# A delta-rule branch whose score matrices are kept in one orientation, the later token's factor moved into level masks and into the small substitutions

## What is computed

```
lhs = I + beta[l] * (k[l] . k[m]) * decay(l, m)     for l later than m, else 0 off the diagonal
sol = lhs^-1 [ beta * v | beta * gamma * k ]        (unit lower triangular solve)
u   = u0 - w @ state
o   = gamma * (q @ state) + (qk * decay) @ u
state = gamma_last * state + kd^T @ u
```

## Time and profile before

| | us |
|---|---|
| median of 3 runs | 805.44 |
| lowest, highest | 804.22, 806.6 |
| the profiled execution | 806.24 |
| its span, first to last instruction | 804.4 |
| PE busy | 748.4 (93%) |
| DVE, ACT, POOL busy | 341.6, 256.1, 300.7 |
| mean granted TensorE clock | 0.996 |

### The profile page before, as it was taken

How to read it: one execution, slowest core, us unless ns; L and a number is a source line. 1 busy time by engine, 2 the same in 40 slices (tenths; PEclk the granted TensorE clock), 3 DMA queues, 4 the chain that set the end, 5 groups by cost and what they waited for, 6 DMA issues and landing times.

```text
span 804.4 us, 14079 instructions
## 1 busy us (share of the span) xinstructions
PE 748.4 (93%) x5523; PEld 598.3 (74%) x5523; DVE 341.6 (42%) x805; ACT 256.1 (32%) x462; POOL 300.7 (37%) x346
## 2 busy tenths in 40 slices
PE   5999999999999999999999999979999999988784
PEld 5887788788878877888888887857767776665551
DVE  6466643285684861435415333651222112211125
ACT  5343232361633767322305255511111111111012
POOL 2774525441520452254444254333333333322111
PEclk9999999999999999999999999999999999999998
DMA  9956742510220522474385294499999999999975
GB/s 250 162 110 124 218 124 53 104 42 13 53 53 20 136 56 53 98 216 96 83 176 169 60 320 183 180 358 375 390 385 389 390 393 387 380 386 387 390 300 219
DMA packets 74346, 166.60 MB, mean 207 GB/s; under 512 B 18838, under 2 KB 46310, under 8 KB 66344
## 3 DMA queue, kind: packets, MB, share of 16 engines
q1 hardware_dynamic: 65856, 150.34, 58.9%
q0 software_dynamic: 5392, 9.61, 3.6%
q10 hardware_dynamic: 3032, 5.74, 2.3%
HBM read 156.98 MB, written 16.97 MB: 216 GB/s over the span
## 4 chain that ended last, share of the span: by engine, by line
PE 58%; DMA 26%; DVE 9%; issue 2%; POOL 2%; ACT 1%; SPq 1%; ACTq 0%; DVEq 0%; POOLq 0%
DMA arena<-in_w_exp_up 24%; PE bank L1075 13%; PE bank L1077 12%; PE bank L1076 12%; PE bank L1068 12%; PE bank L1424 3%; DMA arena<-y_half 1%; PE bank L1434 1%; PE bank L1116 1%; DVE rows L1864 1%; DVE rows L1863 1%; PE bank L1226 1%; DVE h_lo L1836 1%; DVE hT L1908 1%; DMA rt<-in_norm_ffn_g 1%
## 5 line engine op out<-in xcount | busy, mean ns | idle before, releaser
L876 POOL TENSOR_TENSOR ring_low<-ring,w_high 128x512 fp32r<-128x512 f32 (+1 forms) x64 | 81.4, 1272 | 117.2 <-ACT w_high L1516 113.1
L1075 PE MATMUL bank<-h_hi,w_high 128*128 128x512 f32 x296 | 119.5, 404 | 0.0
L1076 PE MATMUL bank<-h_lo,w_high 128*128 128x512 f32 x296 | 115.8, 391 | 0.0
L1424 PEld LDWEIGHTS bank<-arena,hT 128*64 128x64 f32 x1728 | 96.6, 136 | 24.7 <-issue 12.5
L1424 PE MATMUL bank<-arena,hT 128*64 128x128 f32 x1728 | 100.7, 274 | 8.7 <-DMA arena<-in_w_exp_up 6.7
L876 POOL TENSOR_TENSOR w_low<-ring,w_high 128x512 fp32r<-128x512 f32 x56 | 75.9, 1355 | 59.1 <-ACT w_high L1516 54.9
L2182 DVE SCALAR_TENSOR_TENSOR rt<-rt,bank 128x128 f32<-128x128 f32 x32 | 9.2, 288 | 175.3 <-ACT rt L1749 175.3
L1516 ACT ACTIVATE w_high<-ring 128x2048 fp32r<-128x2048 f32 (+1 forms) x32 | 58.7, 1836 | 58.5 <-PE bank L1077 39.3
L1077 PE MATMUL bank<-h_hi,ring_low 128*128 128x512 f32 x168 | 66.6, 396 | 0.0
L1075 PEld LDWEIGHTS bank<-h_hi,w_high 128*128 128x128 f32 x296 | 55.7, 188 | 14.5 <-issue 3.5
L1076 PEld LDWEIGHTS bank<-h_lo,w_high 128*128 128x128 f32 x296 | 55.7, 188 | 11.0
(11 more groups left out here) (330 smaller groups left out, 1313.8 us busy)
## 6 DMA issues: line engine op xcount, KB each, us to landing
arena<-in_w_exp_gate SPq DMA_DIRECT2D x27, 1024.0 KB, 13.3
arena<-in_w_exp_up SPq DMA_DIRECT2D x27, 1024.0 KB, 17.0
arena<-in_w_exp_down SPq DMA_DIRECT2D x27, 1024.0 KB, 19.2
ring<-in_w_in SPq DMA_DIRECT2D x33, 512.0 KB, 6.6
ring<-in_w_exp_gate SPq DMA_DIRECT2D x5, 1024.0 KB, 13.8
ring<-in_w_exp_up SPq DMA_DIRECT2D x5, 1024.0 KB, 17.3
ring<-in_w_exp_down SPq DMA_DIRECT2D x5, 1024.0 KB, 20.5
xres<-in_x SPq DMA_DIRECT2D x8, 512.0 KB, 7.2
```

Source lines behind the costliest of these rows:

```text
L876: after(pool.tensor_tensor(low, full, high, ALU.subtract), w_lo if kk == KD - 2 else step["pool"])
L1075: pe.matmul(o, l_hi, r_hi, start=(n == 0), stop=False)
L1076: pe.matmul(o, l_hi, r_lo, start=False, stop=False)
L1424: ins = pe.matmul(bank[CAP * half:CAP * half + CAP, 1, P * n:P * n + P], xgT[:, x, kk, :], w[:, kk, P * half:P * half + P], start=(kk == 0 ...
```

## The change

`tA` and `tAT` are gone. The scaled scores are never turned: `kk` is written straight to `at` without the later token's factor, which is put back in two places. For the diagonal blocks, `invert_blocks` turns the small table of factors (one more transpose, 128x32) and multiplies the turned blocks by it (one more product of 512 elements a partition) before the substitution. The substitution now reads its columns 32 elements apart instead of next to each other. For the levels, the rows of `P` are the later tokens, so ACT makes masks already multiplied by the factor: two levels, two chunks, four heads, 16 copies of 128x128 a pair, at the odd chunk's `tv`, into `a` and `bgk`. The third level multiplies by the factor where it copied. The three fillers after `kk` and fourteen after `tv` become eighteen after `tv`.

```
 def pieces_after(job):
-    if k in ("kk", "tv") and job[1] % 2:
-        return 3 if k == "kk" else 14
+    if k == "tv" and job[1] % 2:
+        return 18
...
-        for kind in ("G", "kk", "tA", "qk", "tk", "tAT", "tv"):
+        for kind in ("G", "kk", "qk", "tk", "tv"):
...
+        scaled_mask, system_scale = [work["a"], work["bgk"]], rt[:, 960:992]
...
                     if c >= 2:
-                        job_done(pool, ("tAT", c - 2))
+                        job_empty(pool, ("P", c - 2, 0))
...
                     if k == "P" and job[2] == 0:
-                        job_empty(pe, ("tAT", c))
                         pe.wait_ge(x0_ready, c + 1)
...
-                if k == "tA":
-                    act.wait_ge(a_ready, c + 1)
+                if k == "kk":
+                    act.wait_ge(ap_ready, c + 1)
...
-                        copy(by_column[own], work["a"][own, b, :, own], diagonal_ready if lo == P - TURN else step["act"])
-                if k == "tAT":
-                    copy(work["at"][:, c % 2], oh4, e)
+                        copy(by_column[own], work["at"][own, b, :, own], diagonal_ready if lo == P - TURN else step["act"])
...
                 if k == "tv":
...
                     tell(e)
+                    for level in range(2) if c % 2 else ():
+                        if (c, level) == (1, 1):
+                            act.wait_ge(zero_out, 16)
+                        for own in (c - 1, c):
+                            if c > 1:
+                                job_empty(act, ("P", own - 2, level))
+                            for h in range(B_HEADS):
+                                n = 4 * own + h
+                                copy(scaled_mask[level][:, own % 2, h], const(K_LEVEL + level), mask_ready if h == 3 else step["act"], scale=s_bk[:, n:n + 1])
...
                 after(nc.vector.transpose(turned_rows[:, 0:4 * 256], four_times))
+                scales = s_bk[:, 8 * pair:8 * pair + 8].rearrange("p (o s) -> p o s", o=1).to_broadcast([P, 4, 2 * B_HEADS])
+                after(nc.vector.transpose(system_scale, scales))
...
+                after(tt(in_systems, in_systems, by_row_scale, ALU.mult))
...
-                    column = own_block[:, :, :, 33 * j + 1:33 * j + 1 + n].to_broadcast([P, 4, 2, n])
+                    column = own_block[:, :, :, 33 * j + TURN:33 * j + TURN * n + 1:TURN].to_broadcast([P, 4, 2, n])
...
-                    b, dst, dec = c % 2, *(("x", "a") if k == "kk" else ("aqk", "e"))
+                    b, dst, dec = c % 2, *(("at", "a") if k == "kk" else ("aqk", "e"))
...
-                if k == "tA":
-                    for h in range(B_HEADS):
-                        ins = stt(out=work["a"][:, c % 2, h], in0=oh4[:, h], scalar=s_bk[:, 4 * c + h:4 * c + h + 1], in1=ident, op0=ALU.mult, op1=ALU.subtract)
...
                     if k == "P" and width == HALF:
-                        after(nc.vector.tensor_copy(work["p"][HALF:P, b, :, 0:HALF], half_bank(o, job[2])[HALF:P, :, 0]), e)
+                        after(tt(work["p"][HALF:P, b, :, 0:HALF], half_bank(o, job[2])[HALF:P, :, 0], per_head(s_bk, job[1], HALF)[HALF:P], ALU.mult), e)
                     elif k == "P":
-                        after(tt(work["p"][:, b], oh4, over_heads(const(K_LEVEL + job[2])), ALU.mult), e)
+                        dve.wait_ge(mask_ready, 4 * (job[1] // 2) + 2 * job[2] + b + 1)
+                        after(tt(work["p"][:, b], oh4, scaled_mask[job[2]][:, b], ALU.mult), e)
```

More of the change, by code:

```diff
@@ L196 @@
 SOFTMAX_AT = {("gb", 1): 0, ("sc", 2, 0): 1, ("sc", 3, 0): 2, ("gb", 5): 3}
-ON_ACT = {"o2", "tAT", "tk", "tv", "u", "ty", "ga", "gb", "pt", "pv", "aq", "ak", "av", "cq", "xs", "xp"}
+ON_ACT = {"o2", "tk", "tv", "u", "ty", "ga", "gb", "pt", "pv", "aq", "ak", "av", "cq", "xs", "xp"}
 COPIED_BY_DVE = (("xp", 2, 0), ("xp", 3, 0))
@@ L538, in program @@
         ap_ready = sem("ap_ready")
-        a_ready = sem("a_ready")
+        mask_ready = sem("mask_ready")
         diagonal_ready, x0_ready = sem("diagonal_ready"), sem("x0_ready")
@@ L1228, in emit @@
                     return ins
-                if k in ("G", "kk", "qk", "tA", "tk", "tAT", "tv", "ks", "u", "o1", "o2", "S", "ty", "P", "PX"):
+                if k in ("G", "kk", "qk", "tk", "tv", "ks", "u", "o1", "o2", "S", "ty", "P", "PX"):
                     c, b = job[1], job[1] % 2
@@ L1235, in emit @@
                         "kk": [(silu_ready, 12)], "qk": [(silu_ready, 12)], "tk": [(silu_ready, 12)], "tv": [(silu_ready, 12)],
-                        "tA": [(ap_ready, c + 1)], "tAT": [(a_ready, c + 1)], "ks": [(state_ready, c)],
+                        "ks": [(state_ready, c)],
                         "o2": [(aqk_ready, c + 1)], "ty": [(y_ready, c + 1)],
@@ L1275, in emit @@
                         }
-                        turn = {"tA": lambda: w["x"][:, h], "tAT": lambda: w["a"][:, h], "tk": lambda: qkv[:, 4 + h, tok],
+                        turn = {"tk": lambda: qkv[:, 4 + h, tok],
                                 "tv": lambda: qkv[:, 8 + h, tok], "ty": lambda: zs[:, c, h]}
@@ L1857, in invert_blocks @@
                 after(nc.vector.transpose(turned_rows[:, 0:4 * 256], four_times))
+                scales = s_bk[:, 8 * pair:8 * pair + 8].rearrange("p (o s) -> p o s", o=1).to_broadcast([P, 4, 2 * B_HEADS])
+                after(nc.vector.transpose(system_scale, scales))
+                in_systems = turned_rows.rearrange("p (u c) -> p u c", u=2)[:, :, 0:TURN * BLOCK].rearrange("p u (j i) -> p u j i", i=TURN)[:, :, :, 0:BLOCK]
+                by_row_scale = system_scale.rearrange("p (u j o) -> p u j o", u=2, o=1).to_broadcast([P, 2, BLOCK, BLOCK])
+                after(tt(in_systems, in_systems, by_row_scale, ALU.mult))
                 own_block = turned_rows.rearrange("p (o u c) -> p o u c", o=1, u=2)
@@ L2004, in _ @@
                         invert_blocks(c // 2)
-                if k == "tA":
-                    for h in range(B_HEADS):
-                        ins = stt(out=work["a"][:, c % 2, h], in0=oh4[:, h], scalar=s_bk[:, 4 * c + h:4 * c + h + 1], in1=ident, op0=ALU.mult, op1=ALU.subtract)
-                        mark(ins) if h < 3 else after(ins, a_ready)
-                    tell(e)
                 if k in ("P", "PX"):
```

## The result

The changed kernel takes **814.07 us** (median of 4 runs, 812.98 to 816.19), the kernel before beside it 804.83 (4 runs, 804.14 to 806.6). The ratio is 1.0106, with a 95% interval of 1.0086 to 1.0126: slower by 9.2 us, and 1.4 us above the predicted time. The profiled execution is the slowest of the four, 816.19 us with a span of 814.4.

A forecast was written before the change was run, and what follows sets the result against it. PE, busy 93% of the span, bounds the kernel. First pair +2.3, second pair +2.6, end of the chain -1.0 and clock +3.4 sum to +7.3 us: 812.7 us median, 8-in-10 range 807.3 to 816.8.

The forecast's parts named there:

- the sum: Whole kernel: both pairs' delays, the end of the chain and the clock add to +7.3 us, 812.7 us on the median.
- PE's work: First pair: without the turns PE's fillers begin at 161.36, 5.2 us earlier; sixteen of eighteen last to 172.5.
- ACT: First pair: sixteen mask copies of 402 ns take 6.9 us, to 177.3, and delay the tanh's end to 177.9.
- The stalls: PE waits for ACT's tanh in both pairs, 5.6 and 6.0 us; the pairs lose 2.3 and 2.6 us.
- The end of the chain: After the last chunk's u, fillers are used up, so fewer stand around o2: -1.0 us.
- The clock: Behind both stalls PE resumes at the lower clock, 1.7 us a stall: +3.4 us.
- The rival with the clock up: Both stalls come, but the clock does not fall within them, or only at their end: +3.9 us, 809.3; chance 0.22.
- DVE: First pair's substitution: starts at about 163.9, gives the first x at 175.1 and the turned xt by 177.3.
- That rival: DVE's strided reads in the substitution: twice as long, some 3.4 us, x at 178.5, costing some 0.3 us a pair.
- Masks covered, and faster: Masks ready before the seventeenth filler, P starts with x at 175.15 in the first pair: 4.2 us less, 801.2; chance 0.06.
- The masks on DVE: Alternative outside the sum: four 128x512 products, 2.8 us a pair, in place of 6.9 on ACT; no stalls.
- The delay absorbed: Between 258 and 535 us a PE wait for an independent transfer hides part: within 2.4 us of no change.

The follow-up runs named there:

- the second experiment, the clock alone: The changed kernel with 22 extra products of 128x512 (results unused) ahead of the filler that waits, in both pairs: 809.40 us, ratio 1.0057.
- the zeroed low parts: Changed kernel with masks behind the gate tanhs, twelve extra products ahead of each first P, POOL's low-part subtractions replaced by zeroing memsets: 802.82 us, ratio 0.9972.

## Why the prediction was right

The direction, the mechanism and the sum were right: 812.7 forecast, 814.07 measured, inside the range. By its steps:

- **PE's work.** `qk` to 159.0, the last turns at 160.82 (160.95 predicted), fillers from 161.24. Right.
- **ACT.** Sixteen masks at 430 ns from one to the next, 170.66 to 177.57, tanh to 178.2. Predicted were 170.4, 177.3 and 177.9. One mask takes 402 ns by the lines of the profile, as the exponential of the earlier trace rows did: it was the right row to take.
- **The stalls.** 5.6 and 6.0 us predicted, 5.66 and 6.00 measured, and their place and releaser as named. Their worth, 2.3 + 2.6 - 1.0 = 3.9 us, came out as 4.10 in the run where the clock stayed up.
- **The end of the chain.** The delay shrinks from 9.50 us at the second pair's `PX` (231.73 before, 241.23 after) to 8.42: -1.1, predicted -1.0.
- **The clock.** The direction from the earlier trace rows was right, the size was the mis-sized term: 1.7 us a stall predicted, 2.6 and 1.65 measured. That is 4.3 us in place of 3.4. The middle between nothing and 3.4 had no row behind it, so that it came this close is in part luck. The first pair's 0.50 lasted from before PE resumed until about 184, through both fillers and both `P`; in the second pair it was back at 0.87 from 238 to 240, as `P` began. The prediction quoted the Trainium skill, TensorE: Matmul & The Clock Gate, section on the HAM clock gate, by which the clock is throttled by default and released by activity. The trace agrees: in both pairs the higher level came back only after PE was at work again. The rival with the clock up (809.3) is what the second experiment then made: 809.40.
- **DVE.** This step was wrong, and it cost nothing only because ACT was later. I put `x` at 175.1; it was there at 177.4, 2.3 us later. I took 0.7 us for the product of the factors, "half of 1.42", and let the substitution start 2.5 us earlier than in the earlier trace rows without asking what POOL did there. In the kernel before, the first step starts at 167.73, right as POOL's subtractions end at 167.70, and DVE's transposes, which have one input, cover the time until then. Moved ahead, the steps ran into it. Of the 2.3 us this explains 1.6 (0.74 and 0.90, by the rows with the zeroed low parts); the rest is reads 32 elements apart, 0.36 us against 0.28 at 128x112 and less as the steps get shorter, some 0.6 us over fifteen. That rival was right in kind and far below its bound of 3.4.
- **Masks covered, and faster.** The 801.2 of that rival rested on `x` at 175.1. With the masks off the path and the clock kept up the time was 805.93 and 805.64. To go below the kernel before, the collision has to go as well. The masks on DVE, which the prediction priced beside its sum at 2.8 us a pair, were not run.
- **The delay absorbed.** It was not: 8.42 us at the first scores, 8.38 at the first product of the experts' stage.

Against the measured 9.2 us, the stage accounts for 8.4, where the sum had 7.3. The remaining 0.8 lies behind it. In the profiled execution, the slowest of the four, 1.5 us arose there, at PE's wait for the experts' weights.

## What to carry over

When work is moved earlier on one engine, list what the other engines run in the new place: an operation's time from a trace holds only beside the same neighbours. A loop of small copies placed ahead of the one copy for which TensorE waits delays that copy by its whole length, and the kernel pays for what TensorE cannot fill with other work; behind it, the loop cost nothing here; if the pause that is left still lets the clock fall, its price is paid twice. An engine that is set free starts its next work early, which may be where it does most harm. And what a stage gains can be lost again where a later stage waits for its transfers.

## What the runs showed of the hardware

**DVE and POOL exclude each other, when DVE reads two tiles of SBUF and POOL reads too.** Beside POOL's subtractions a DVE product of 128x512 took 1.43 us for 0.69, two of them 2.89 for 1.42, a step of 128x16 1.23 for 0.18, and each ended behind the subtraction beside which it began. A subtraction that began while such a product ran took 1.61 us for 1.30. DVE's transposes (1.25 us for 128x1024) were not lengthened by them, before or after, and its scaled products of `kk` and `qk`, with one input from PSUM, took 1.12 to 1.13 us for four in every run shown. The Trainium skill, SBUF — State Buffer, section Who interferes with whom, says this: the port pair that the two engines share is an exclusive lock, and a DVE instruction with two SBUF inputs contends with a GpSimd instruction that reads SBUF, not with one that only writes it. The first half agrees with these rows. The second, on two-input instructions beside one that only writes, no run here shows.

**A DVE copy can be held up too, even by a memset.** The copy of 128x128 (one input) took 0.23 us in the profile after, where it began between two subtractions. It took 0.70 where it began within one (162.77 to 164.06, with the inclusive mask later) and 0.46 where it began within a memset, and both times it ended within 0.1 us behind POOL's instruction. In the kernel before it began only 0.14 us ahead of the end of a subtraction, and took 0.23.

**How long PE pauses does not settle whether the clock falls.** With half the masks ahead, PE stopped at 224.68 and resumed at 227.24, a pause of 2.56 us. The clock was at 1.00 until 228 and at 0.59 from 228 to 230, with PE at work again; the earlier trace rows had suggested that only pauses of more than 3.5 us matter. A pause of 3.60 us was followed by 0.54. Pauses of 2.22 and 2.33 us ahead of a filler and of `P` were not followed by a fall. Among the experts, in one execution (the clock alone), a wait of 2.29 us left 64 products at 3.77 us, and one of 1.92 us was followed by 0.60 and 5.43 us. In the stall of 14.80 us the clock fell to 0.52 between 228 and 230, stayed at 0.50 until PE had resumed, and came back to 1.00 only 4 us later. Each of these is one profiled execution. That such pauses widen the spread of a kernel is not shown: with half the masks ahead ten runs lie within 4.1 us, and with PE busy and the inclusive mask later eleven lie within 4.0.
